# Retention's values centred per token, in place of a mean taken over the retention output

## The chip, the cores and the metric

The kernel runs on one core of a Trainium2 chip, as one launch. The metric is the device time in microseconds (us) of that core. The engines are named as in the profile: PE (TensorE), with PEld for its weight loads, DVE (VectorE), ACT (ScalarE), POOL (GpSimd) and SP (SyncE, which here only issues DMAs).

## The reference

Two decoder blocks over 512 tokens of width 1024, all in float32. The first has a retention layer, a chunked attention layer and two MLPs with a squared ReLU, the second a layer with three kinds of attention and a gated MLP. The change touches the retention layer only, which has 4 heads of key width 256 and value width 512:

```
q, k, v, g = split(h @ w_in)            # per head: q, k 512x256; v, g 512x512
q, k = rope(q), rope(k) / sqrt(256)
o = decayed_scores(q, k) @ v            # per head 512 tokens x 512 values; chunkwise in the reference
mu  = mean(o, axis=-1)                  # over the 512 values of a head, per token
var = mean((o - mu)**2, axis=-1)
o = (o - mu) * rsqrt(var + 1e-6) * gn_g
y = (silu(g) * o) @ w_out
```

Each output token is a weighted sum of value rows, so the mean of an output row over its 512 values is the same weighted sum of the means of the value rows.

## The kernel before

Matrix products are float32 in accuracy: each operand is rounded to a high part (hi) and the rest (lo), and each product is three matmuls, hi by hi, hi by lo and lo by hi (lines 590 to 592, `mm3`). The weights come from one stream of 354 units of 128x1024 floats, in a ring of four slots. SP loads a unit into `raw`, ACT rounds it into `w_hi` (L1189), DVE subtracts it into `w_lo` (L1753); this pair is called `split`, and it is done three units ahead of the unit that PE works on. Each engine has its program written out by hand in its own order; only semaphores tie them together. Engines work strictly in the order of their programs.

Projections make tiles of 128 features by 512 tokens that go to PSUM banks 0 and 1 in turn. PE may start a tile only when the tile two before it has been read (semaphore `tile_read`). V is made the other way round (`token_major`): 128 tokens by 512 values of a head, in banks 4 to 7.

The order of a retention head `ret_head` on PE is: four tiles for Q and K; four units of V; the output projection of the head before (`ret_out`, four units of two tiles each; the first head has none, the last has two here and two later); the four score products; the first tile of the gate G; P by V (L745 on) into banks 4 to 7; the other three tiles of G. With heads 1 and 2 in a loop and heads 0 and 3 written out.

Around V: when V stands in banks 4 to 7, ACT rounds each bank, scaled by the token's inverse norm (`rcol`), into `rv_h` (L1290, 4 instructions), and DVE makes `rv_l` from the bank and `rv_h` (L1912, 4 instructions). Behind these stands the next `split` of each engine, and behind that, on DVE, `out_tile`, which adds a tile of the output projection to `h` (L1811) and gives `tile_read`. The scores' third product uses bank 4 and so waits for `v_lo`; in head 0 it is P by V that waits for `v_lo`. P is rounded by ACT (L1298) and POOL takes its lo part (L2706). The semaphore `ret_p_lo` tells PE that POOL is done.

Around the group norm: ACT copies P by V from the banks to `oc` (L1308). POOL adds the four tiles of `oc` (L2711, L2715); inside the third gate tile PE multiplies that sum by a 128x128 matrix of ones (L759), which spreads the total over all partitions; DVE subtracts 1/512 of it from the four tiles of `oc` (L1933); ACT squares them into `sq` (L1314); POOL adds the squares (L2711, L2715 again); inside the fourth gate tile PE reduces them to a column per 128 tokens (L765); DVE and ACT make the inverse root (L1938, L1320, L1941, `make_diag` L1796 to L1801), PE spreads it (`gn_spread`, L658, L659) and DVE scales and gates (`y_scale` L1830, `y_gate` L1835).

Of the kernel before, what the change touches and what calls it, by code (L numbers as in the profile page):

```python
# [230 lines left out]
def build(nc, stream, x_t, cols, wf, f_bias, sinks, rel_pad, rel_2, c_rope, c_decay, c_sq, c_tri, c_sel,  # L231
# [4 lines left out]
    with ExitStack() as ctx:  # L236
# [38 lines left out]
        def f32(ap):  # L275
            return ap.bitcast(F32)
# [18 lines left out]
        m2, r_first = small[:, 2, 8:12], small[:, 2, 12:16]  # L295
        fl, fe, fn = small[:, 8, :], small[:, 9, :], small[:, 10, :]
        flog = small[:, 11, :]
        sums2 = [small[:, 4, 8 + 4 * n:12 + 4 * n] for n in range(2)]


# [36 lines left out]
        first_spread = sem("first_spread")  # L337
        h_normed = sem("h_normed")

        rope_tables = sem("rope_tables")  # L340
        rope_ready = sem("rope_ready")
        rope_hi = sem("rope_hi")
        rope_lo = sem("rope_lo")
        v_hi = sem("v_hi")
        v_lo = sem("v_lo")
        decay_landed = sem("decay_landed")
        ret_scores = sem("ret_scores")
        ret_p = sem("ret_p")
# [3 lines left out]
        ret_o = sem("ret_o")  # L352
        gn_sum = sem("gn_sum")
        gn_done = sem("gn_done")
        gn_centred = sem("gn_centred")
        gn_sq = sem("gn_sq")
        gn_ms_r = sem("gn_ms_r")
        gn_sd_r = sem("gn_sd_r")
# [71 lines left out]
        merge_a = sem("merge_a")  # L430
        merged = sem("merged")

        pad_made = sem("pad_made")
        conv_0 = sem("conv_0")
        conv_1 = sem("conv_1")
        conv_2 = sem("conv_2")
# [146 lines left out]
        def _(pe):  # L583
# [126 lines left out]
            def ret_head(hd, first, last=False):  # L710
                if first:
                    token_major(0, tiles=xl_ready)
                    strip_rows()
                    token_major(1, tiles=xl_ready)
                    proj(first=[(xl_ready, 0)], hooks={7: first_square})
                    proj(hooks={4: lambda: spread_rms(0)})
                else:
                    proj(hooks={5: lambda: gn_spread(hd - 1)})
                    proj()
                proj()  # L720
                proj()

                wait(pe, ret_o, hd * 4)
                for kk in range(2 if first else 0, 4):
                    token_major(kk)
                if not first:
                    wait(pe, y_lo, hd * 4)
                    for n in range(2 if last else 4):
                        ret_out(n)

                wait(pe, rope_lo, hd * 4 + 4)
                narrow = 1 if first else 4
                assert not first or at.t.b % 2 == 0
                if first:
                    wait(pe, tile_read, at.t)
                for j, (b, o) in enumerate([(2, 0), (3, 0), (narrow, 0), (narrow, 256)]):
                    if j == 2 and not first:
                        wait(pe, v_lo, hd * 4 + 4)
                    for d in range(2):
                        keys = (rqk_h[2 + d][:, j * P:j * P + P], rqk_l[2 + d][:, j * P:j * P + P])  # L740
                        m = mm3(banks[b][:, o:o + T_W[j]], keys, (rqk_h[d][:, j * P:S], rqk_l[d][:, j * P:S]),
                                d == 0, d == 1)
                    m.then_inc(ret_scores, 1)
                proj()

                if first:
                    wait(pe, v_lo, hd * 4 + 4)
                wait(pe, ret_p_lo, hd * 4 + 4)
                for c in range(4):
                    for j in range(TT):  # L750
                        val = (rv_h[j][:, c * P:c * P + P], rv_l[j][:, c * P:c * P + P])
                        sc = (rp_h[:, T_AT[j]:T_AT[j] + T_W[j]], rp_l[:, T_AT[j]:T_AT[j] + T_W[j]])
                        m = mm3(banks[4 + c][:, j * P:S], val, sc, j == 0, j == TT - 1)
                    m.then_inc(ret_pv, 1)
                proj()

                def mean():
                    wait(pe, gn_sum, hd * 6 + 3)
                    pe.matmul(banks[2][:, :], ones[:, :], acc[:, :], start=True, stop=True).then_inc(gn_done, 1)  # L759

                def variance():

                    wait(pe, gn_sum, hd * 6 + 6)
                    for t in range(TT):
                        m = pe.matmul(banks[3][:, t:t + 1], acc[:, t * P:t * P + P], ones[:, 0:1],  # L765
                                      start=True, stop=True)
                    m.then_inc(gn_done, 1)

                proj(hooks={3: mean})
                proj(hooks={6: variance})  # L770
                if last:
                    ret_out(2, hook=lambda: gn_spread(hd))
                    ret_out(3)
# [397 lines left out]
        def _(act):  # L1171
# [97 lines left out]
            def ret_head(hd, first, last=False):  # L1269
# [17 lines left out]
                value_splits(2 if first else 4)  # L1287
                wait(act, products_done, at.pe)
                for t in range(TT):
                    act.activation(rv_h[t], banks[4 + t][:, :], ACT.Copy, scale=rcol[:, t:t + 1]).then_inc(v_hi, 1)  # L1290
                if not first:
                    for _ in range(2 if last else 4):
                        split()
# [2 lines left out]
                for j in range(4):  # L1296
                    wait(act, ret_p, hd * 4 + (j + 1))
                    act.activation(rp_h[:, T_AT[j]:T_AT[j] + T_W[j]], pf_ret[:, T_AT[j]:T_AT[j] + T_W[j]],  # L1298
                                   ACT.Copy).then_inc(ret_p_hi, 1)
                at.step()  # L1300
                gate(hd, 0)
                split()
# [7 lines left out]
                gate(hd, 1)  # L1310
                split()
                for c in range(4):
                    wait(act, gn_centred, hd * 4 + (c + 1))
                    act.activation(sq[:, c, :], oc[c], ACT.Square).then_inc(gn_sq, 1)  # L1314
                at.step()
                gate(hd, 2)
# [419 lines left out]
        def _(dve):  # L1736
# [105 lines left out]

            def y_of(hd):

                wait(dve, gn_done, hd * 3 + 3)
                y_scale(hd, 0)
                y_scale(hd, 1)
                wait(dve, gate_ready, hd * 4 + 4)
                y_gate(hd, 0)
                y_scale(hd, 2)  # L1850
                y_gate(hd, 1)
                y_scale(hd, 3)
                y_gate(hd, 2)
                y_gate(hd, 3)
# [26 lines left out]
            def ret_head(hd, first, last=False):  # L1881
# [3 lines left out]
                if first:  # L1885
                    dve.wait_ge(squares_landed, 16)
                    rms(0)
                    dve.wait_ge(rbc_ready, 1)
                    dve.wait_ge(rope_landed, 32)
                    dve.tensor_tensor(cosr, cosr, rbc[:, :], ALU.mult)  # L1890
                    dve.tensor_tensor(sinr, sinr, rbc[:, :], ALU.mult).then_inc(rope_tables, 1)
                    dve.wait_ge(rope_tables, 1)

                    dve.wait_ge(masks_ready, 1)
                at.step()
# [12 lines left out]
                rotate(hd, 1, 1)  # L1908
                value_splits(2 if first else 4)
                for t in range(TT):  # L1910
                    wait(dve, v_hi, hd * 4 + (t + 1))
                    dve.scalar_tensor_tensor(rv_l[t], banks[4 + t][:, :], rcol[:, t:t + 1], f32(rv_h[t]),  # L1912
                                             ALU.mult, ALU.subtract).then_inc(v_lo, 1)
                if not first:
                    for n in range(2 if last else 4):
                        split()
# [9 lines left out]
                                      decay[:, 0:T_W[j]], ALU.mult).then_inc(ret_p, 1)  # L1926
                for c in range(4):
                    split()
                    if c == 2:

                        wait(dve, gn_done, hd * 3 + 1)
                        for e in range(4):
                            dve.scalar_tensor_tensor(oc[e], banks[2][:, :], -1.0 / RV, oc[e],  # L1933
                                                     ALU.mult, ALU.add).then_inc(gn_centred, 1)
                    if c == 3:

                        wait(dve, gn_done, hd * 3 + 2)
                        dve.tensor_scalar(gn_ms, banks[3][:, 0:4], 1.0 / RV, EPS, ALU.mult, ALU.add)\  # L1938
                            .then_inc(gn_ms_r, 1)
                        wait(dve, gn_sd_r, hd + 1)  # L1940
                        dve.reciprocal(gn_r, gn_sd).then_inc(gn_r_r, 1)  # L1941
                        wait(dve, gn_r_r, hd + 1)
                        make_diag(gn_r, gn_diag_h, gn_diag_l, gn_split, hd + 1).then_inc(gn_diag, 1)
                    at.step()
                    scaled(sg[c]).then_inc(tile_read, 1)
                if last:
                    split()
                    out_tile(4)
                    wait(dve, gn_done, hd * 3 + 3)
                    y_scale(hd, 0)  # L1950
                    y_scale(hd, 1)
                    wait(dve, gate_ready, hd * 4 + 4)
# [573 lines left out]

            for n in range(4):
                m = dve.memset(cz[n][:, 0:2], 0.0)
            m.then_inc(pad_made, 1)
            dve.wait_ge(pad_made, 1)  # L2530

            def taps(pair, n):

# [114 lines left out]
        def _(pool):  # L2648
# [45 lines left out]
            def ret_head(hd, first):  # L2694
# [11 lines left out]
                    pool.tensor_tensor(rp_l[:, a:a + w], pf_ret[:, a:a + w], f32(rp_h[:, a:a + w]), ALU.subtract)\  # L2706
                        .then_inc(ret_p_lo, 1)

                for k, (src, ready) in enumerate(((oc, ret_o), ([sq[:, c, :] for c in range(4)], gn_sq))):
                    wait(pool, ready, hd * 4 + 2)  # L2710
                    pool.tensor_tensor(acc[:, :], src[0], src[1], ALU.add).then_inc(gn_sum, 1)  # L2711
                    for c in (2, 3):
                        wait(pool, ready, hd * 4 + (c + 1))
                        wait(pool, gn_sum, hd * 6 + (3 * k + c - 1))
                        pool.tensor_tensor(acc[:, :], acc[:, :], src[c], ALU.add).then_inc(gn_sum, 1)  # L2715

            ret_head(Lin(0), True)
            with pool.Fori(0, RH - 1) as i:
# [290 lines left out]
```

## Time and profile before

| what | value |
|---|---|
| median of three runs | 2106.79 us (2106.16 to 2106.81) |
| the profiled execution, its own time | 2105.78 us |
| its span in the trace | 2104.1 us |
| PE busy | 2080.5 us, 99% of the span |
| DVE, ACT, POOL busy | 67%, 46%, 16% |
| the retention layer in the trace | from the start to about 421 us |

The span is what the trace covers; the execution's own time is 1.7 us longer. A timeline row gives start and duration in us, the engine, the line, the operation, the tiles written and read, and how long the engine had been idle before it and on whose account. A matmul's duration in the trace (0.39 us for 512 columns) overlaps that of the next one; the distance between two starts is what it costs.

### The profile page before, as it was taken

The page shows a single profiled execution, that of the slowest core. Times are in us where ns is not written, and L with a number is a line of the kernel's source. Part 1 is how long each engine was busy: PE and PEld are TensorE (multiplying, and loading weights), DVE is VectorE, ACT ScalarE, POOL GpSimd, SP SyncE. Part 2 cuts the span into 40 slices and gives each one's busy share as a digit, 9 for nine tenths or more (in the row PEclk, how much of TensorE's full clock was granted, in tenths as well). Part 3 has the DMA queues.
Part 4 walks back from the last instruction along what each step waited for, and adds up shares of the span by engine and source line. Part 5 has one row for each costly group of instructions (what it writes and reads, how often), then busy time and mean ns, then how long its engine had stood idle before and what let it go on. Part 6 is the DMA issues. An engine that isn't in the chain of part 4 may idle for free.

```text
span 2104.1 us, 30452 instructions
## 1 busy us (share of the span) xinstructions
PE 2080.5 (99%) x10614; PEld 1770.9 (84%) x10614; DVE 1403.4 (67%) x2320; ACT 978.2 (46%) x1652; POOL 330.1 (16%) x351
## 2 busy tenths in 40 slices
PE   8999999999999999999999999999999999999998
PEld 6888888789989888887899898878888888888887
DVE  6565554677868753887778687667765456666674
ACT  4433333464554344786645543457652244433342
POOL 4223132210001111443100002312310010000001
PEclk9999999999999999999999999999999999999999
DMA  5222213224234232222132232221222222333232
GB/s 195 84 92 76 100 65 100 70 71 155 99 106 146 97 104 85 91 90 76 61 131 90 100 112 99 96 90 53 76 83 100 100 90 96 109 103 113 99 104 67
DMA packets 58549, 203.77 MB, mean 97 GB/s; under 512 B 6937, under 2 KB 9129, under 8 KB 58448
## 3 DMA queue, kind: packets, MB, share of 16 engines
q1 hardware_dynamic: 54304, 189.82, 26.9%
q0 software_dynamic: 3712, 11.95, 1.9%
q8 instruction: 64, 1.05, 0.2%
q10 hardware_dynamic: 432, 0.66, 0.1%
q14 instruction: 37, 0.30, 0.0%
HBM read 200.27 MB, written 6.06 MB: 98 GB/s over the span
## 4 chain that ended last, share of the span: by engine, by line
PE 93%; ACT 3%; DVE 3%; issue 1%; DMA 0%; POOL 0%; ACTq 0%; DVEq 0%
PE bank L590 29%; PE bank L592 29%; PE bank L591 29%; PE bank L884 1%; PE bank L863 1%; ACT arena L1463 1%; PE bank L899 1%; PE bank L897 1%; DVE w_lo L1753 1%; PE bank L864 1%; ACT w_hi L1189 1%; ACT arena_r L1482 0%; ACT arena_r L1471 0%; DVE h L1811 0%; DMA colv<-in_cols 0%
## 5 line engine op out<-in xcount | busy, mean ns | idle before, releaser
L590 PE MATMUL bank<-x_hi,w_hi 128*128 128x512 f32 x1552 | 610.9, 394 | 1.4 <-issue 0.7
L591 PE MATMUL bank<-x_lo,w_hi 128*128 128x512 f32 x1560 | 608.0, 390 | 0.0
L592 PE MATMUL bank<-x_hi,w_lo 128*128 128x512 f32 x1552 | 605.3, 390 | 0.0
L1753 DVE TENSOR_TENSOR w_lo<-raw,w_hi 128x1024 fp32r<-128x1024 f32 x306 | 409.1, 1341 | 240.6 <-ACT w_hi L1189 240.3
L590 PE MATMUL bank<-arena_r,w_hi 128*128 128x256 f32 (+1 forms) x1328 | 440.1, 331 | 1.5 <-DVE h L1811 1.1
L592 PE MATMUL bank<-arena_r,w_lo 128*128 128x256 f32 (+1 forms) x1328 | 438.8, 330 | 0.0
L591 PE MATMUL bank<-arena_r,w_hi 128*128 128x256 f32 (+1 forms) x1312 | 432.6, 330 | 0.0
L1189 ACT ACTIVATE w_hi<-raw 128x1024 fp32r<-128x1024 f32 x306 | 320.0, 1051 | 192.6 <-PE bank L592 188.9
L590 PEld LDWEIGHTS bank<-x_hi,w_hi 128*128 128x128 f32 x1552 | 291.9, 188 | 62.4 <-issue 2.0
L591 PEld LDWEIGHTS bank<-x_lo,w_hi 128*128 128x128 f32 x1560 | 293.5, 188 | 60.2 <-issue 1.0
L592 PEld LDWEIGHTS bank<-x_hi,w_lo 128*128 128x128 f32 x1552 | 291.6, 188 | 61.5
L590 PEld LDWEIGHTS bank<-arena_r,w_hi 128*128 128x128 f32 x1328 | 252.4, 190 | 28.1 <-issue 2.9
L592 PEld LDWEIGHTS bank<-arena_r,w_lo 128*128 128x128 f32 x1328 | 252.4, 190 | 23.2
L591 PEld LDWEIGHTS bank<-arena_r,w_hi 128*128 128x128 f32 x1312 | 249.4, 190 | 22.3
L2750 POOL TENSOR_SCALAR arena<-arena,small 128x256 f32<-128x256 f32 (+3 forms) x128 | 89.5, 711 | 237.8 <-DVE small L2248 192.3
L1806 DVE TENSOR_TENSOR arena<-bank,rbc 128x512 f32<-128x512 f32 x77 | 53.0, 688 | 96.1 <-PE bank L592 96.0
L1811 DVE TENSOR_TENSOR h<-bank,h 128x512 f32<-128x512 f32 x96 | 65.6, 686 | 69.0 <-PE bank L592 68.9
L590 PE MATMUL bank<-w_hi,x_hi 128*128 128x512 f32 x224 | 88.2, 394 | 10.2 <-DVE x_lo L1759 9.3
L1359 ACT ACTIVATE w_hi<-raw 128x512 fp32r<-128x512 f32 x96 | 58.7, 623 | 77.8 <-PE bank L592 66.0
L1684 ACT ACTIVATE arena<-arena,colv 128x512 f32<-128x512 f32 x44 | 35.9, 817 | 124.6 <-DVE arena L1806 124.6
L2082 DVE TENSOR_TENSOR arena<-bank,arena 128x256 f32<-128x256 f32 x186 | 75.5, 417 | 23.4 <-PE bank L592 22.0
L591 PE MATMUL bank<-w_lo,x_hi 128*128 128x512 f32 x224 | 87.9, 393 | 0.0
(269 smaller groups left out, 2525.2 us busy)
## 6 DMA issues: line engine op xcount, KB each, us to landing
raw<-in_stream SPq DMA_DIRECT2D x354, 512.0 KB, 3.2
arena<-in_rel_pad POOLq DMA_DIRECT2D x16, 256.0 KB, 3.7
bias_strips<-bias_strip_once POOLq DMA_DIRECT2D x12, 320.0 KB, 4.3
out_t<-h SPq DMA_DIRECT2D x8, 256.0 KB, 2.2
h<-in_x_t SPq DMA_DIRECT2D x6, 256.0 KB, 8.4
arena<-in_c_decay POOLq DMA_DIRECT2D x4, 256.0 KB, 3.0
arena<-bias_strips POOLq DMA_DIRECT2D x4, 256.0 KB, 3.7
arena<-bias_strips POOLq DMA_DIRECT2D x8, 128.0 KB, 2.4
```

The source lines that it names most:

```text
L590: pe.matmul(dst, lh, rh, start=start, stop=False, **kw)
L591: pe.matmul(dst, lh, rl, start=False, stop=False, **kw)
L592: return pe.matmul(dst, ll, rh, start=False, stop=stop, **kw)
L863: pe.matmul(dst, q, kh_st[half][:, k0:k0 + w], start=True, stop=False, skip_group_check=True)
L1189: act.activation(w_hi[:, u % RING, :], raw[:, u % RING, :], ACT.Copy).then_inc(hi_ready, 1)
L1359: act.activation(block_at(slot)[0], src, ACT.Copy).then_inc(done, 1)
L1684: act.activation(cy[2 * (pair.b % 2) + n], cz[2 * (pair.b % 2) + n][:, 2:S + 2], ACT.Identity, scale=col(k + (C_CW + 2 * 2 * PAIRS)), bias ...
L1753: dve.tensor_tensor(w_lo[:, s, :], raw[:, s, :], f32(w_hi[:, s, :]), ALU.subtract).then_inc(lo_ready, 1)
L1806: return dve.tensor_tensor(dst, banks[(at.t - 1) % 2][:, :], rbc[:, :], ALU.mult)
L1811: dve.tensor_tensor(h[:, j, :], banks[(at.t - 1) % 2][:, :], h[:, j, :], ALU.add).then_inc(tile_read, 1)
L2082: dve.tensor_tensor(part, banks[bank][:, 0:QUARTER], part, ALU.add).then_inc(quarter_read, 1)
L2750: pool.tensor_scalar(pf[par][:, a:a + w], pf[par][:, a:a + w], rinv[par][:, t:t + 1], 1.0, ALU.mult, ALU.mult).then_inc(sm.probs, 1)
```

## The change

V is centred before it is rounded. ACT first copies each scaled bank of V to `sq` and has the instruction give the sum of each row as well (`accum_out`, into `v_sum`). DVE multiplies the sum by -1/512 (`v_neg`, one small instruction for each of the four token tiles). ACT then adds `v_neg` as a bias and rounds `sq` to `rv_h`, and DVE makes `rv_l` from `sq`, `v_neg` and `rv_h`. In heads 1 to 3 both follow at once. In head 0 ACT does it behind its rounding of P, and DVE behind the `split` of the first gate tile.

In the group norm the mean product on PE, POOL's three sums of `oc` and DVE's four subtractions go; ACT's squares stand where they stood and take `oc` as it was copied from the banks. The other edits only rename or recount semaphores.

```diff
@@ PE, ret_head
-                def mean():
-                    wait(pe, gn_sum, hd * 6 + 3)
-                    pe.matmul(banks[2][:, :], ones[:, :], acc[:, :], start=True, stop=True).then_inc(gn_done, 1)
...
-                    wait(pe, gn_sum, hd * 6 + 6)
+                    wait(pe, gn_sum, hd * 3 + 3)
...
-                proj(hooks={3: mean})
+                proj()
                 proj(hooks={6: variance})
@@ ACT, ret_head
                 for t in range(TT):
-                    act.activation(rv_h[t], banks[4 + t][:, :], ACT.Copy, scale=rcol[:, t:t + 1]).then_inc(v_hi, 1)
+                    act.activation(sq[:, t, :], banks[4 + t][:, :], ACT.Copy, scale=rcol[:, t:t + 1],
+                                   accum_out=v_sum[:, t:t + 1]).then_inc(v_scaled, 1)
+
+                def centred_his():
+                    for t in range(TT):
+                        wait(act, v_mean, hd * 4 + (t + 1))
+                        act.activation(rv_h[t], sq[:, t, :], ACT.Identity, bias=v_neg[:, t:t + 1]).then_inc(v_hi, 1)
+
+                if not first:
+                    centred_his()
                 if not first:
                     for _ in range(2 if last else 4):
                         split()
...
+                if first:
+                    centred_his()
                 at.step()
                 gate(hd, 0)
...
-                    wait(act, gn_centred, hd * 4 + (c + 1))
+                    wait(act, ret_o, hd * 4 + (c + 1))
                     act.activation(sq[:, c, :], oc[c], ACT.Square).then_inc(gn_sq, 1)
@@ DVE, ret_head
                 for t in range(TT):
-                    wait(dve, v_hi, hd * 4 + (t + 1))
-                    dve.scalar_tensor_tensor(rv_l[t], banks[4 + t][:, :], rcol[:, t:t + 1], f32(rv_h[t]),
-                                             ALU.mult, ALU.subtract).then_inc(v_lo, 1)
+                    wait(dve, v_scaled, hd * 4 + (t + 1))
+                    dve.tensor_scalar(v_neg[:, t:t + 1], v_sum[:, t:t + 1], -1.0 / RV, None, ALU.mult).then_inc(v_mean, 1)
+
+                def centred_los():
+                    for t in range(TT):
+                        wait(dve, v_hi, hd * 4 + (t + 1))
+                        dve.scalar_tensor_tensor(rv_l[t], sq[:, t, :], v_neg[:, t:t + 1], f32(rv_h[t]),
+                                                 ALU.add, ALU.subtract).then_inc(v_lo, 1)
+
+                if not first:
+                    centred_los()
...
                 for c in range(4):
                     split()
-                    if c == 2:
-
-                        wait(dve, gn_done, hd * 3 + 1)
-                        for e in range(4):
-                            dve.scalar_tensor_tensor(oc[e], banks[2][:, :], -1.0 / RV, oc[e],
-                                                     ALU.mult, ALU.add).then_inc(gn_centred, 1)
+                    if c == 0 and first:
+                        centred_los()
@@ POOL, ret_head
-                for k, (src, ready) in enumerate(((oc, ret_o), ([sq[:, c, :] for c in range(4)], gn_sq))):
-                    wait(pool, ready, hd * 4 + 2)
-                    pool.tensor_tensor(acc[:, :], src[0], src[1], ALU.add).then_inc(gn_sum, 1)
-                    for c in (2, 3):
...
+                wait(pool, gn_sq, hd * 4 + 2)
+                pool.tensor_tensor(acc[:, :], sq[:, 0, :], sq[:, 1, :], ALU.add).then_inc(gn_sum, 1)
+                for c in (2, 3):
...
```

## Rows read from the trace of the kernel before

**Rows 1.** The page: busy time of each engine.

```profile
PE 2080.5 (99%) x10614; PEld 1770.9 (84%) x10614; DVE 1403.4 (67%) x2320; ACT 978.2 (46%) x1652; POOL 330.1 (16%) x351
```

**Rows 2.** The waits of PE, whole span: us in total, times, longest.

```profile
PE bank L590 <- DVE x_lo L1759: 9.3, 1, 9.3
...
PE bank L1138 <- DVE diag L2615: 1.1, 1, 1.1
```

**Rows 3.** Timeline of PE around the mean product, head 0.

```profile
83.17 0.40 PE L592 MATMUL bank<-x_hi,w_lo 128*128 128x512 f32 x1
83.40 1.02 PE L759 MATMUL bank<-acc,ones 128*128 128x512 f32 x2
...
84.73 0.40 PE L592 MATMUL bank<-x_hi,w_lo 128*128 128x512 f32 x1
```

**Rows 4.** Timeline of ACT and of DVE behind V, head 1.

```profile
138.34 2.42 ACT L1290 ACTIVATE arena_r<-bank,small 128x512 fp32r<-128x512 f32 x4 [4.38 <-PE bank L592]
140.63 1.08 ACT L1189 ACTIVATE w_hi<-raw 128x1024 fp32r<-128x1024 f32 x1
...
141.74 1.23 DVE L1753 TENSOR_TENSOR w_lo<-raw,w_hi 128x1024 fp32r<-128x1024 f32 x1
142.88 0.68 DVE L1811 TENSOR_TENSOR h<-bank,h 128x512 f32<-128x512 f32 x1
```

**Rows 5.** Timeline of PE, the same stretch: second to third tile of `ret_out`.

```profile
143.35 0.39 PE L592 MATMUL bank<-arena_r,w_lo 128*128 128x512 f32 x1
143.71 0.47 PE L590 MATMUL bank<-arena_r,w_hi 128*128 128x512 f32 x1
```

**Rows 6.** Timeline of ACT in the attention layer: activations with accumulator output.

```profile
827.26 0.72 ACT L1463 ACTIVATE arena<-arena,small 128x512 f32<-128x512 f32 x1 [3.26 <-DVE small L2223]
827.89 0.18 ACT L1463 ACTIVATION_READ_ACCUMULATOR arena<-arena,small 128x1 f32 x1
827.98 0.60 ACT L1463 ACTIVATE arena<-arena,small 128x384 f32<-128x384 f32 x1
```

**Rows 7.** Timeline of ACT and of DVE behind the last output tiles.

```profile
410.67 0.73 ACT L1196 ACTIVATE x_hi<-h,colv 128x512 fp32r<-128x512 f32 x1
411.30 0.62 ACT L1204 ACTIVATE sq<-h 128x512 f32<-128x512 f32 x1
...
409.30 0.73 DVE L1759 SCALAR_TENSOR_TENSOR x_lo<-h,colv,x_hi 128x512 fp32r<-128x512 f32 x1
409.96 0.67 DVE L1811 TENSOR_TENSOR h<-bank,h 128x512 f32<-128x512 f32 x1
```

**Rows 8.** Timeline of POOL, DVE and PE, head 0, P's lo part.

```profile
64.90 2.00 POOL L2706 TENSOR_TENSOR arena_r<-arena,arena_r 128x384 fp32r<-128x384 f32 x1
66.85 1.15 POOL L2706 TENSOR_TENSOR arena_r<-arena,arena_r 128x256 fp32r<-128x256 f32 x2
...
63.82 2.20 DVE L1753 TENSOR_TENSOR w_lo<-raw,w_hi 128x1024 fp32r<-128x1024 f32 x1
...
68.15 0.47 PE L590 MATMUL bank<-arena_r 128*128 128x512 f32 x1
```

**Rows 9.** Timeline of POOL, head 1, the same operation.

```profile
164.45 1.02 POOL L2706 TENSOR_TENSOR arena_r<-arena,arena_r 128x384 fp32r<-128x384 f32 x1
```

**Rows 10.** Timeline of DVE, last head: centring, then the third gate tile.

```profile
377.66 2.48 DVE L1933 SCALAR_TENSOR_TENSOR arena<-bank,arena 128x512 f32<-128x512 f32 x4
380.52 0.69 DVE L1806 TENSOR_TENSOR arena<-bank,rbc 128x512 f32<-128x512 f32 x1 [0.38 <-PE bank L592]
```

**Rows 11.** Timeline of PE, the first matmuls of the kernel.

```profile
9.34 0.77 PE L590 MATMUL bank<-w_hi,x_hi 128*128 128x512 f32 x1 [9.34 <-DVE x_lo L1759]
...
13.30 0.39 PE L590 MATMUL bank<-w_hi,x_hi 128*128 128x512 f32 x1
13.53 0.40 PE L591 MATMUL bank<-w_lo,x_hi 128*128 128x512 f32 x1
```

**Rows 12.** Stages: busy us (instructions) of PE, PEld, DVE, ACT, POOL, then granted clock, DMA.

```profile
10.00:15.00 5.00, 5.00 (x17) 3.94 (x16) 4.54 (x4) 5.00 (x9) 4.29 (x3) 1.00 1.04 400
```

More of the change, by code:

```diff
@@ L297, in build @@
         flog = small[:, 11, :]
+        v_sum, v_neg = small[:, 8, 0:4], small[:, 9, 0:4]
         sums2 = [small[:, 4, 8 + 4 * n:12 + 4 * n] for n in range(2)]
@@ L338, in build @@
         h_normed = sem("h_normed")
-        rope_tables = sem("rope_tables")
+        tables_made = sem("tables_made")
         rope_ready = sem("rope_ready")
@@ L345, in build @@
         v_lo = sem("v_lo")
+        v_scaled = sem("v_scaled")
+        v_mean = sem("v_mean")
         decay_landed = sem("decay_landed")
@@ L354, in build @@
         gn_done = sem("gn_done")
-        gn_centred = sem("gn_centred")
         gn_sq = sem("gn_sq")
@@ L431, in build @@
         merged = sem("merged")
-        pad_made = sem("pad_made")
         conv_0 = sem("conv_0")
@@ L1843, in y_of @@
             def y_of(hd):
-                wait(dve, gn_done, hd * 3 + 3)
+                wait(dve, gn_done, hd * 2 + 2)
                 y_scale(hd, 0)
@@ L1890, in ret_head @@
                     dve.tensor_tensor(cosr, cosr, rbc[:, :], ALU.mult)
-                    dve.tensor_tensor(sinr, sinr, rbc[:, :], ALU.mult).then_inc(rope_tables, 1)
-                    dve.wait_ge(rope_tables, 1)
+                    dve.tensor_tensor(sinr, sinr, rbc[:, :], ALU.mult).then_inc(tables_made, 1)
+                    dve.wait_ge(tables_made, 1)
                     dve.wait_ge(masks_ready, 1)
@@ L1928, in ret_head @@
                     split()
-                    if c == 2:
-                        wait(dve, gn_done, hd * 3 + 1)
-                        for e in range(4):
-                            dve.scalar_tensor_tensor(oc[e], banks[2][:, :], -1.0 / RV, oc[e],
-                                                     ALU.mult, ALU.add).then_inc(gn_centred, 1)
+                    if c == 0 and first:
+                        centred_los()
                     if c == 3:
-                        wait(dve, gn_done, hd * 3 + 2)
+                        wait(dve, gn_done, hd * 2 + 1)
                         dve.tensor_scalar(gn_ms, banks[3][:, 0:4], 1.0 / RV, EPS, ALU.mult, ALU.add)\
@@ L1948, in ret_head @@
                     out_tile(4)
-                    wait(dve, gn_done, hd * 3 + 3)
+                    wait(dve, gn_done, hd * 2 + 2)
                     y_scale(hd, 0)
@@ L2528, in _ @@
                 m = dve.memset(cz[n][:, 0:2], 0.0)
-            m.then_inc(pad_made, 1)
-            dve.wait_ge(pad_made, 1)
+            m.then_inc(tables_made, 1)
+            dve.wait_ge(tables_made, 2)
             def taps(pair, n):
@@ L2707, in ret_head @@
                         .then_inc(ret_p_lo, 1)
-                for k, (src, ready) in enumerate(((oc, ret_o), ([sq[:, c, :] for c in range(4)], gn_sq))):
-                    wait(pool, ready, hd * 4 + 2)
-                    pool.tensor_tensor(acc[:, :], src[0], src[1], ALU.add).then_inc(gn_sum, 1)
-                    for c in (2, 3):
-                        wait(pool, ready, hd * 4 + (c + 1))
-                        wait(pool, gn_sum, hd * 6 + (3 * k + c - 1))
-                        pool.tensor_tensor(acc[:, :], acc[:, :], src[c], ALU.add).then_inc(gn_sum, 1)
+                wait(pool, gn_sq, hd * 4 + 2)
+                pool.tensor_tensor(acc[:, :], sq[:, 0, :], sq[:, 1, :], ALU.add).then_inc(gn_sum, 1)
+                for c in (2, 3):
+                    wait(pool, gn_sq, hd * 4 + (c + 1))
+                    wait(pool, gn_sum, hd * 3 + (c - 1))
+                    pool.tensor_tensor(acc[:, :], acc[:, :], sq[:, c, :], ALU.add).then_inc(gn_sum, 1)
             ret_head(Lin(0), True)
```

## The prediction

> **What bounds the kernel now.** I read the page's busy times first: PE is busy for 99% of the span, DVE for 67% [rows 1]. So a change is worth what it does to PE's program, and nothing that the other engines save counts unless PE waits for them. The waits of PE come next [rows 2]: after the 9.3 us at the start no single wait is over 1.1 us. That view can't show how near PE is to waiting where it doesn't wait. For that I read the timeline of each engine around the places that the diff touches.
>
> A matmul of 512 columns starts 0.23 us after the one before it (13.30 to 13.53) [rows 11]. At the third tile of `ret_out` the distance is 0.36 us, 143.35 to 143.71 [rows 5], so PE was held for 0.13 us. This tile may start when DVE has added the first one, and that addition ran from 142.88 to 143.56 [rows 4]. PE followed 0.15 us after its end. The profile calls this gap "issue", but the times fit `tile_read`: behind V, DVE is only just in time. Heads 2 and 3 run the same program, and I take them to be alike. Whatever delays DVE's first addition here delays PE by as much.
>
> **The mean product, removed.** From the L592 before it to the L592 behind it there are 1.56 us, in which three ordinary steps take 0.69 [rows 11]; the product costs PE 0.87 us [rows 3]. Four heads: **3.5 us gained**. The two records of L759 last 1.02 us; the price is not this duration but what the distance between starts leaves.
>
> **The three sums and four subtractions, removed.** The subtractions take DVE 2.48 us, and behind them DVE still waits 0.38 us for PE before it reads the third gate tile [rows 10]. PE hides them; taking them away gives nothing. If they were not hidden they would be worth up to 4 times 2.5 us, but then DVE would not be idle behind them. POOL is 16% busy, and the mean product started with no wait on POOL [rows 3]: nothing either. The fourth gate tile's reduction stays where it is, so the long chain through the inverse root starts at the same point of PE's program.
>
> **V in heads 1 to 3, in two passes.** I take head 1. ACT begins at 138.34; four copies last until the next instruction at 140.63, 0.57 us each [rows 4]. Now:
>
> - An accumulator output brings a second instruction. With it the next activation starts 0.72 us after the first [rows 6], where one of the same size with a pointer operand and no accumulator has a pitch of 0.63 (410.67 to 411.30) [rows 7]. It adds 0.09, so the scaled copies take 4 times 0.66, to 141.00.
> - The centring pass is four more activations from SBUF with a pointer operand, at 0.63 [rows 7], to 143.52. DVE's small products lie between and are hidden: the first is wanted 2 us after its sum exists.
> - ACT's split of the next unit starts then, and DVE's part follows 1.11 us after its start, as before (140.63 to 141.74), at 144.63. DVE's four low parts have two SBUF operands now and go at the pitch of such an instruction, 0.66 us (409.30 to 409.96) [rows 7]; the first can start when the first `rv_h` stands, 141.72, so they end at 144.4 and are ready just before the split.
> - DVE's split takes 1.14 us to the next start, the addition 0.68, and PE follows 0.15 later [rows 4, 5]: 146.60 in place of 143.71.
>
> The stall grows by **2.9 us** in each of three heads, 8.7 us. Later in the head it does not come again: the second addition follows at once, before PE has ended the third tile, and the splits are three units ahead. The scores' wait for `v_lo` is far behind in heads 1 and 2; in head 3 two units of `ret_out` (48 steps of 0.23, 11 us) still lie in front of it. The DMA queue is not held: the slot that SP fills waits on a split of an earlier unit.
>
> The bounds. Lower: the accumulator is free and the second pass is as quick as the first, 0.57. Then DVE's low parts end last, at 144.0, and PE starts at 146.0, 2.3 us late. Upper: nothing overlaps, each copy costs 0.72 + 0.18 and each centring 0.72; ACT's split then starts at 144.8, and PE is 4.2 us late. I take 2.9, as the rows with pointer operand and accumulator are the same instruction with another function.
>
> **V in head 0.** Here no `ret_out` covers it; P by V starts at 68.15, when POOL has the low parts of P (66.85 + 1.15 = 68.00) [rows 8]. The new low parts of V come behind DVE's split, from about 65.95. But DVE and POOL do not run side by side here: the split took 2.20 us where it takes 1.23 elsewhere [rows 4, 8], and POOL's 384 columns took 2.00 us where they take 1.02 in head 1 [rows 9]. One waits while the other works. From 65.95 on POOL has 0.95 + 1.15 us left and DVE four times 0.66; one after the other, in whatever order, the last ends at about 70.7, and PE starts at 70.85. **2.7 us lost.** If the two shared freely, DVE would end at 68.65 and the loss were 0.7; that is the lower bound, and 3.3 us the upper, if each change of hands costs 0.1 to 0.2 more.
>
> The Trainium skill (SBUF — State Buffer, the section "SBUF: two separate sides") says that a VectorE operation with two SBUF inputs and a GpSimd operation that reads SBUF lock each other out for the whole instruction. By that rule the old low part, with one input in PSUM, was free of it, and the new one is not: head 0 loses 2.7 us, and without the rule 0.7. The two stretched rows agree with it.
>
> **The sum.** -3.5 + 8.7 + 2.7 = +7.9 us. On the profiled execution's own 2105.78 us (span 2104.1 and 1.7 around it) that is 2113.7; the median of the runs shown lies 1.0 above that execution, so **2114.7 us**, 0.38% slower. With the lower bounds -3.5 + 6.9 + 0.7 = +4.1, 2110.9; with the upper ones -3.5 + 12.6 + 3.3 = +12.4, 2119.2.
>
> **Rivals.** *The third tile is not held by DVE.* The profile itself says "issue" for the 0.13 us; if PE's gate is something else, or DVE's addition goes ahead sooner, the second pass is hidden in heads 1 to 3. Place: the third tile of `ret_out`; the point from which it decides is a first addition that ends within 5.2 us of V's first copy. Then the time is 2106.8 - 3.5 + 2.7 = 2106.0, or 2103.3 if head 0's is hidden too. Against it: the step is longer than the 0.23 of its neighbours just there, and begins where the addition ends [rows 4, 5]. 1 in 10.
>
> *The clock of PE falls after the new gaps.* Nowhere behind the start has PE been idle for longer than 1.1 us [rows 2], and four gaps of 2.7 to 3 us would be new. At the start, after 9.3 us of idleness, nine steps take 3.96 us (9.34 to 13.30), 0.44 each, about what 512 columns take at 1.2 GHz, and from then on 0.23, at 2.4 GHz; the granted clock reads 1.00 in that stage all the same [rows 11, 12]. In place of 2.07 us, that is 1.9 us lost. Four times that gives 2114.7 + 7.6 = 2122.3. Gaps longer than 1.1 us are not in this trace behind the start. The Trainium skill (TensorE: Matmul & The Clock Gate, the table under "Why this matters for your kernels") warns that idle gaps between bursts of matmuls, of about the length forecast here, throw TensorE back to the lower clock; this would bring the 2122.3. No row here shows it. 7 in 100.
>
> *The stall lies between the two.* Say DVE gains an order in which half of the pass is hidden: below 2110.9 and above 2106. 3 in 100.
>
> **Numbers.** The forecast has 80 in 100 with its bounds 2110.9 to 2119.2, and with that I leave 2 in 10 outside. A measurement of this kernel tells 0.2% (4.2 us) from no change. Slower by that means above 2111.0: the forecast and the clock, 0.85. Same: most of the first rival and the third, 0.12. Faster needs less than 2102.6, more than the removed products are worth, 0.03.
>
> **What the profile after would show.** The waits of PE: L590 for DVE's L1811, three times some 2.9 us, and one of some 2.7 us at the start of P by V in head 0, for DVE's or POOL's low parts. No rows of the mean product, and 0.23 us steps across the third gate tile. ACT's group behind V about 5.2 us long where it was 2.4, with accumulator reads of 0.18. In head 0, low parts of V stretched or alternating with POOL's. The step between matmuls behind the gaps says whether the clock held. The prediction is wrong if the addition L1811 comes as early as before, if the second pass overlaps the first, or if the matmuls behind a gap are 0.43 us apart.

## The result, and the profile after

The changed kernel takes 2112.66 us (median of six runs, 2112.0 to 2117.93), against 2106.22 us for the kernel before in the runs beside it: the ratio is 1.0037, with a 95% interval of 1.0027 to 1.0048. It is slower, by 6.4 us in the medians. The span of the profiled execution grew from 2104.1 to 2110.6 us, by 6.5.

The waits of PE after show where. Each row has the time in all, the number of waits, and the longest (the lines have moved: L1819 is the addition to `h`, L1925 the low part of V, L1761 and L1186 the two halves of a split, L1287 and L1293 the two passes of ACT over V):

```profile
PE bank L591 <- DVE h L1819: 9.4, 6, 2.8
...
PE bank L591 <- DVE arena_r L1925: 1.7, 1, 1.7
```

The additions' row in the kernel before was

```profile
PE bank L590 <- DVE h L1811: 1.1, 3, 0.4
```

It now has three waits more, of 2.8 us each. The row of L1925 is new. The mean product had no row in this view even before: what it cost was PE's own work, not a wait, so its removal can't be seen here.

The timeline of ACT, DVE and PE behind V in head 1 answers to [rows 4, 5]:

```profile
138.92 0.69 ACT L1287 ACTIVATE sq<-bank,small 128x512 f32<-128x512 f32 x1 [4.38 <-PE bank L593]
139.51 0.19 ACT L1287 ACTIVATION_READ_ACCUMULATOR sq<-bank,small 128x1 f32 x1
139.60 0.68 ACT L1287 ACTIVATE sq<-bank,small 128x512 f32<-128x512 f32 x1
...
141.59 2.56 ACT L1293 ACTIVATE arena_r<-sq,small 128x512 fp32r<-128x512 f32 x4
144.05 2.00 ACT L1186 ACTIVATE w_hi<-raw 128x1024 fp32r<-128x1024 f32 x2
...
142.35 2.74 DVE L1925 SCALAR_TENSOR_TENSOR arena_r<-sq,small,arena_r 128x512 fp32r<-128x512 f32 x4 [0.46 <-ACT arena_r L1293]
145.13 1.23 DVE L1761 TENSOR_TENSOR w_lo<-raw,w_hi 128x1024 fp32r<-128x1024 f32 x1
146.27 1.28 DVE L1819 TENSOR_TENSOR h<-bank,h 128x512 f32<-128x512 f32 x2
...
143.94 0.39 PE L593 MATMUL bank<-arena_r,w_lo 128*128 128x512 f32 x1
147.10 0.47 PE L591 MATMUL bank<-arena_r,w_hi 128*128 128x512 f32 x1 [2.78 <-DVE h L1819]
```

Read it from ACT down. The pitch of a scaled copy is 0.66 or 0.67 us (138.92, 139.60) where it was 0.57; the second pass goes from 141.59 to 144.05; only then comes the split, then DVE's half of it, then the addition, and PE starts its third tile at 147.10. That is 8.18 us behind V's first copy, where it was 5.37 (138.34 to 143.71) [rows 4, 5]: 2.81 us more. This time the profile names the addition as the releaser. Heads 2 and 3 show the same gap of 2.78 us.

Behind the last of the three gaps there is more. PE in head 3, and the granted clock over stretches around it (the columns are those of [rows 12]):

```profile
353.25 0.47 PE L591 MATMUL bank<-arena_r,w_hi 128*128 128x512 f32 x1 [2.78 <-DVE h L1819]
...
354.51 0.63 PE L593 MATMUL bank<-arena_r,w_lo 128*128 128x512 f32 x1
354.94 0.63 PE L591 MATMUL bank<-arena_r,w_hi 128*128 128x512 f32 x1
...
357.90 0.40 PE L592 MATMUL bank<-arena_r,w_hi 128*128 128x512 f32 x1
```

```profile
346.00:350.00 4.00, 4.00 (x19) 3.33 (x18) 2.00 (x7) 4.00 (x10) 0.00 (x0) 1.00 0.00 0
353.00:358.00 5.00, 4.75 (x14) 3.78 (x15) 2.09 (x4) 0.00 (x0) 0.00 (x0) 0.66 0.64 212
358.00:362.00 4.00, 4.00 (x20) 3.31 (x19) 1.12 (x2) 1.06 (x1) 0.00 (x0) 1.00 0.00 1
```

From 354.51 to 357.90 the steps are 0.43 us, 512 columns at 1.2 GHz, and the granted clock is 0.66 over the stretch from 353 to 358; then they are 0.23 again. Ten steps from 354.02 to 357.90 took 3.88 us in place of 2.3: the clock cost 1.6 us here. Behind the other two gaps it held. The kernel before had such a fall too, at a place where PE had no gap, in the second block, behind a run of one-column matmuls:

```profile
1350.32 0.58 PE L652 MATMUL bank<-ones,arena 128*128 128x1 f32 x4
1350.77 0.47 PE L590 MATMUL bank<-x_hi,w_hi 128*128 128x512 f32 x1
...
1351.31 0.63 PE L592 MATMUL bank<-x_hi,w_lo 128*128 128x512 f32 x1
1351.74 0.63 PE L590 MATMUL bank<-x_hi,w_hi 128*128 128x512 f32 x1
```

The trace after has no fall there. So in these two traces a fall of 1.6 us stands on each side. At this place the clock fell in five of the nine traces (the kernel before and, of the experiments below, V's part alone, head 0's low parts ahead of the split, half of the passes moved, and the low parts from the bank) and held in the other four, though the change and the experiments leave this part of the program as it was.

### The profile page after: what moved, and what is told of

Its sections match the earlier page's. It is cut to its first block, busy times and chain, and to the rows that moved or that the text cites. A ratio compares the mean times of both kernels' runs of the same rounds, so it can differ in the third digit from the quotient of the medians.

```text
span 2110.6 us, 30442 instructions
## 1 busy us (share of the span) xinstructions
PE 2077.6 (98%) x10606; PEld 1769.0 (84%) x10606; DVE 1395.1 (66%) x2320; ACT 987.8 (47%) x1684; POOL 315.5 (15%) x339
## 4 chain that ended last, share of the span: by engine, by line
PE 93%; ACT 3%; DVE 3%; issue 1%; DMA 0%; POOL 0%; DVEq 0%; ACTq 0%
PE bank L591 29%; PE bank L593 29%; PE bank L592 29%; PE bank L881 1%; PE bank L860 1%; PE bank L896 1%; DVE w_lo L1761 1%; PE bank L861 1%; PE bank L894 1%; ACT w_hi L1186 1%; ACT arena L1471 1%; ACT sq L1287 1%; ACT arena_r L1293 0%; DVE h L1819 0%; ACT arena_r L1490 0%
## 5 line engine op out<-in xcount | busy, mean ns | idle before, releaser
L1761 DVE TENSOR_TENSOR w_lo<-raw,w_hi 128x1024 fp32r<-128x1024 f32 x306 | 406.4, 1332 | 239.3 <-ACT w_hi L1186 238.9
L1186 ACT ACTIVATE w_hi<-raw 128x1024 fp32r<-128x1024 f32 x306 | 319.6, 1051 | 193.5 <-PE bank L593 190.2
L1819 DVE TENSOR_TENSOR h<-bank,h 128x512 f32<-128x512 f32 x96 | 65.5, 687 | 72.5 <-PE bank L593 72.4
```

What stands on the lines that cost most here:

```text
L1186: act.activation(w_hi[:, u % RING, :], raw[:, u % RING, :], ACT.Copy).then_inc(hi_ready, 1)
L1761: dve.tensor_tensor(w_lo[:, s, :], raw[:, s, :], f32(w_hi[:, s, :]), ALU.subtract).then_inc(lo_ready, 1)
L1819: dve.tensor_tensor(h[:, j, :], banks[(at.t - 1) % 2][:, :], h[:, j, :], ALU.add).then_inc(tile_read, 1)
```

## The experiments

All times are medians beside runs of the kernel before on the same chip, 2105.91 us; ratios have their 95% interval.

**The group norm's part alone.** The kernel before, less everything that the change takes from the group norm:

```diff
-                proj(hooks={3: mean})
+                proj()
...
-                        for e in range(4):
-                            dve.scalar_tensor_tensor(oc[e], banks[2][:, :], -1.0 / RV, oc[e],
-                                                     ALU.mult, ALU.add).then_inc(gn_centred, 1)
```

> The kernel before, without the mean product on PE, without POOL's three sums of oc and without DVE's four subtractions. V is not centred either, so this kernel leaves out the centring of the group norm. My theory: only the product lay on PE's path, 0.87 us in each of 4 heads, so -3.5 us, about 2102.7 (ratio 0.9983), with the step between matmuls at 0.23 us across the third gate tile. Rival: DVE's 2.5 us of subtractions and POOL's sums were not wholly covered; then it gains more than 3.5 us, up to 4 x 3.4 = 13 us.

Measured: 2102.15 us, ratio 0.9982 (0.9973 to 0.9991), 3.8 us less. PE walks through the third gate tile without a step longer than 0.23:

```profile
84.13 0.39 PE L592 MATMUL bank<-x_hi,w_lo 128*128 128x512 f32 x1
84.36 0.39 PE L590 MATMUL bank<-x_hi,w_hi 128*128 128x512 f32 x1
84.58 0.39 PE L591 MATMUL bank<-x_lo,w_hi 128*128 128x512 f32 x1
```

The 3.5 us of the product are there, and the subtractions and sums are worth nothing that can be told apart from it (the interval is some 2 us wide on each side).

**V's part alone.** The changed kernel with the mean product, the sums and the subtractions put back:

```diff
-                proj()
+                proj(hooks={3: mean})
```

> The kernel after, with the mean product, the sums and the subtractions put back (they then subtract a mean that is zero but for rounding). My theory: all of the loss is in V's second pass: three gaps of 2.8 us on PE and 1.5 us in head 0, +9.9 us, about 2116, and 1.6 us more for each gap after which the clock falls. Rival: the loss comes from what the removal did (squares and sums sooner, other meetings of DVE and POOL); then this kernel is no more than 3.5 us above the one before.

Measured: 2120.21 us, ratio 1.0068 (1.0054 to 1.0082), 14.3 us more. The trace has the same three gaps of 2.78 us and one of 1.65 in head 0, some 10 us in all, and behind two of the three the clock fell; this is the second:

```profile
252.24 0.68 PE L591 MATMUL bank<-arena_r,w_hi 128*128 128x512 f32 x1 [2.78 <-DVE h L1823]
252.72 0.63 PE L592 MATMUL bank<-arena_r,w_hi 128*128 128x512 f32 x1
253.14 0.63 PE L593 MATMUL bank<-arena_r,w_lo 128*128 128x512 f32 x1
```

10.0 + 2 x 1.6 = 13.2, near the 14.3; the span of this trace is 13.6 us longer than that of the kernel before, and each of the two has a fall behind the one-column matmuls besides. The two parts alone, -3.8 and +14.3, make 10.5 where the whole change made 6.4. Falls of the clock explain most of the 4.1 us between them: the mean granted clock is known for every execution, and it is 0.996 in four of these five, where the trace has three falls, and 0.998 in four of the changed kernel's six, where the trace has one. Two falls more are 3.2 us. Why this kernel has them more often isn't known.

**The passes moved behind the first addition.** No work added or taken; in heads 1 to 3 only the order changes:

```diff
@@ ACT
+                if not first:
+                    split()
                 wait(act, products_done, at.pe)
...
@@ DVE
-                if not first:
-                    centred_los()
                 if not first:
                     for n in range(2 if last else 4):
-                        split()
+                        if n:
+                            split()
                         for c in range(2):
                             out_tile(2 * n + c)
+                            if n == 0:
+                                centred_los(range(2 * c, 2 * c + 2))
```

(DVE's first split stands ahead of the `v_neg` products.)

> The kernel after, with one thing moved: in heads 1 to 3 ACT's and DVE's split of the next unit, and the first addition to h, go ahead of the centring passes, whose low parts are then made two behind each of the first two additions. No work is added or taken. My theory: PE's third tile is held by the addition behind the passes, so the three gaps go: 2106.2 - 3.5 + 1.5 = 2104.2 (ratio 0.9990), no PE gap by the addition over 0.2 us in heads 1 to 3, and no fall of the clock there. Rival: PE waits because ACT and DVE have more work in all behind V; then the gaps move to the fourth or fifth tile or to the scores and the time stays near 2112.

Measured: 2103.91 us, ratio 0.9989 (0.9980 to 0.9998). The waits of PE, and PE across the second and third tile in head 1, where the gap was:

```profile
PE bank L591 <- DVE arena_r L1930: 1.6, 1, 1.6
...
PE bank L591 <- DVE h L1822: 1.1, 3, 0.4
```

```profile
143.64 0.39 PE L592 MATMUL bank<-arena_r,w_hi 128*128 128x512 f32 x1
143.87 0.39 PE L593 MATMUL bank<-arena_r,w_lo 128*128 128x512 f32 x1
144.10 0.39 PE L591 MATMUL bank<-arena_r,w_hi 128*128 128x512 f32 x1
144.32 0.39 PE L592 MATMUL bank<-arena_r,w_hi 128*128 128x512 f32 x1
```

The additions' row is back at what it was before the change. The third tile starts at 144.10, 0.23 us behind the step before it, so the hold of 0.13 us that the kernel before had there [rows 5] is gone too. The same passes cost nothing when the addition doesn't stand behind them. The rival that it was the amount of work is out. The traced execution, at 2101.43 us the quickest of the eleven, has no fall of the clock at all (granted clock 0.999); those at 2104 us and more have 0.998 or 0.997.

**In head 0 the low parts ahead of the split.**

```diff
                 for c in range(4):
-                    split()
                     if c == 0 and first:
                         centred_los()
+                    split()
```

> As e3_passes_later, and in head 0 DVE makes the low parts of V ahead of its split. My theory: that split of 1.1 us is taken out of the turns that DVE and POOL take, so P by V starts some 1.1 us sooner: about 2103.1. Rival: POOL's low parts of P end last then, pushed back by DVE, or ACT's rounding of V (its last ends at about 66.4 in the trace after) sets the start; then 0.3 us or less is gained, about 2104.

Measured: 2102.22 us, ratio 0.9982 (0.9973 to 0.9991). DVE and PE in head 0:

```profile
64.87 4.01 DVE L1930 SCALAR_TENSOR_TENSOR arena_r<-sq,small,arena_r 128x512 fp32r<-128x512 f32 x4 [1.24 <-ACT arena_r L1295]
68.81 1.21 DVE L1764 TENSOR_TENSOR w_lo<-raw,w_hi 128x1024 fp32r<-128x1024 f32 x1
...
68.94 0.50 PE L591 MATMUL bank<-arena_r 128*128 128x512 f32 x1 [0.68 <-DVE arena_r L1930]
```

The gap shrinks from 1.64 to 0.68 us, by 1.0 where 1.1 was expected; the low parts could not start until ACT's first `rv_h` stood (DVE idle for 1.24 us). The median fell by 1.7 us, more than the gap did; the executions of the kernel without this step already spread from 2101.4 to 2104.7 us, so of the medians' difference only the gap's 1.0 us is accounted for. This kernel beats both: 3.7 us less than the kernel before, 10 less than the change as made.

**Longer gaps.** One more DVE product behind the low parts, which nobody reads:

```diff
                 if not first:
                     centred_los()
+                    dve.tensor_tensor(f_at(2, 4), f32(x_hi[:, 0:4, :]).rearrange("p k n -> p (k n)"),
+                                      f32(x_lo[:, 0:4, :]).rearrange("p k n -> p (k n)"), ALU.mult)
```

> The kernel after, with one product of 2048 elements more on DVE behind the low parts of V in heads 1 to 3; nobody reads its result. My theory: DVE's first addition comes some 2 us later still, PE's three gaps grow from 2.8 to about 4.8 us, and now the clock falls behind each of the three, 1.6 us each (seven matmuls at 0.43 us in place of 0.23): 2106 - 3.5 + 1.5 + 3 x (4.8 + 1.6) = 2123. Rival: the fall seen in the kernel after has nothing to do with the gap (it stood at another place of the kernel before, with no gap); then the three gaps grow, the clock falls once or not at all in the trace, and the time is 2118 to 2120.

Measured: 2124.16 us, ratio 1.0086 (1.0069 to 1.0102). The first of the three gaps, and the clock before, behind and later:

```profile
150.19 0.77 PE L591 MATMUL bank<-arena_r,w_hi 128*128 128x512 f32 x1 [4.85 <-DVE h L1819]
150.75 0.63 PE L592 MATMUL bank<-arena_r,w_hi 128*128 128x512 f32 x1
151.18 0.63 PE L593 MATMUL bank<-arena_r,w_lo 128*128 128x512 f32 x1
```

```profile
140.00:144.00 4.00, 4.00 (x19) 3.34 (x18) 1.25 (x5) 4.00 (x11) 0.00 (x0) 1.00 0.02 4
150.00:155.00 5.00, 4.82 (x11) 3.80 (x12) 1.77 (x3) 0.00 (x0) 0.00 (x0) 0.50 0.66 210
156.00:160.00 4.00, 4.00 (x19) 3.31 (x18) 1.53 (x3) 1.06 (x1) 0.00 (x0) 1.00 0.00 0
```

All three gaps of 4.85 us are followed by matmuls at the lower level, 10, 6 and 12 records of 0.62 to 0.63 us. These 28 steps cost some 0.2 us each, 5.6 us in all, where I had forecast 4.8. The extra product took DVE 2.2 us, and the gaps grew by 2.07. So a microsecond of DVE here costs PE very nearly a microsecond, and these gaps cost the clock as well, each time.

**Half of the passes moved.** ACT and DVE centre two token tiles ahead of the split and two behind it:

```diff
-                    centred_los()
+                    centred_los(range(2))
...
+                        if n == 0:
+                            centred_los(range(2, 4))
```

> The kernel after, with only two of the four token tiles centred ahead of the split and the first additions in heads 1 to 3, and the other two behind them. My theory: two activations of 0.63 us leave the chain to the first addition, so the gaps shrink from 2.8 to about 1.5 us, and the clock does not fall behind them: 2106 - 3.5 + 1.5 + 3 x 1.5 = 2108.6. Rival: whether a gap is long does not matter to the clock; then some of these gaps too are followed by matmuls at 0.43 us, and the time is 1.6 us more for each.

Measured: 2108.69 us, ratio 1.0014 (1.0004 to 1.0023). Head 1:

```profile
145.70 0.47 PE L591 MATMUL bank<-arena_r,w_hi 128*128 128x512 f32 x1 [1.56 <-DVE h L1821]
146.00 0.40 PE L592 MATMUL bank<-arena_r,w_hi 128*128 128x512 f32 x1
146.24 0.39 PE L593 MATMUL bank<-arena_r,w_lo 128*128 128x512 f32 x1
```

Three gaps of 1.56 us (the third 1.57), none followed by a slow step. With gaps of 1.6, 2.8 and 4.85 us in heads 1 to 3 the clock fell behind none of three, behind three of six (two traces), and behind three of three. Nor did it fall behind head 0's gap of 1.65 us, which five traces have.

**Head 0's low parts from the bank.** The same instruction with one SBUF input instead of two, on top of the kernel with the passes moved:

```diff
+                        if first:
+                            dve.scalar_tensor_tensor(rv_l[t], banks[4 + t][:, :], rcol[:, t:t + 1], f32(rv_h[t]),
+                                                     ALU.mult, ALU.subtract).then_inc(v_lo, 1)
+                            continue
```

> As e3_passes_later, but in head 0 the low parts of V are taken from V's PSUM bank, as in the kernel before (so rv_l of head 0 leaves out the mean; the rest computes as before). The instruction is as long, with one SBUF input in place of two. My theory: with two SBUF inputs DVE and POOL take turns, with one they don't, so the four low parts take 2.7 us in place of 4.2, POOL's four 4.4 in place of 5.3, and PE begins P by V some 1.4 us sooner, nearly without a gap: 2102.6. Rival: head 0's gap is only the order of DVE's work behind its split; then the low parts stay stretched to 4 us, PE's gap stays at 1.6 us, and the time at 2104.

Measured: 2101.65 us, ratio 0.9978 (0.9969 to 0.9988). First DVE and POOL operation by operation in the changed kernel, head 0:

```profile
65.38 1.51 DVE L1925 SCALAR_TENSOR_TENSOR arena_r<-sq,small,arena_r 128x512 fp32r<-128x512 f32 x1
66.81 1.22 DVE L1925 SCALAR_TENSOR_TENSOR arena_r<-sq,small,arena_r 128x512 fp32r<-128x512 f32 x1
...
64.34 2.00 POOL L2718 TENSOR_TENSOR arena_r<-arena,arena_r 128x384 fp32r<-128x384 f32 x1
66.30 1.18 POOL L2718 TENSOR_TENSOR arena_r<-arena,arena_r 128x256 fp32r<-128x256 f32 x1
67.44 0.90 POOL L2718 TENSOR_TENSOR arena_r<-arena,arena_r 128x128 fp32r<-128x128 f32 x1
...
69.61 0.50 PE L591 MATMUL bank<-arena_r 128*128 128x512 f32 x1 [1.65 <-DVE arena_r L1925]
```

and the same stretch with the bank as source:

```profile
65.92 2.71 DVE L1931 SCALAR_TENSOR_TENSOR arena_r<-bank,small,arena_r 128x512 fp32r<-128x512 f32 x4
...
63.61 4.38 POOL L2728 TENSOR_TENSOR arena_r<-arena,arena_r 128x512 fp32r<-128x512 f32 x4 [9.83 <-ACT arena_r L1307]
...
68.69 0.50 PE L591 MATMUL bank<-arena_r 128*128 128x512 f32 x1 [0.19 <-DVE arena_r L1931]
```

Above, each operation is as long as it takes to wait for the other engine's and then do its own: DVE's first low part lasts 1.51 us and ends 0.55 us after POOL's 384 columns (66.34). Below, four low parts take 2.71 us in place of 4.17, and POOL's four 4.38 in place of 5.27. PE's gap falls from 1.65 to 0.19 us. So the turns come from the second SBUF input, not from the order on DVE. (The time fell by 2.3 us against the kernel with the passes moved, more than the 1.45 of the gap; the rest is not traced to a cause.)

## Why the prediction was right

It said 2114.7 us, between 2110.9 and 2119.2; it was 2112.66, 6.4 us slower where 7.9 were forecast.

- *The bound and the edge.* DVE's first addition was the thing to look at, though the wait view had it at nothing. Moving it took the gaps away, and the 0.13 us with them; lengthening the chain by 2 us lengthened them by 2. So the 0.13 us were the wait for the addition, whatever the profile called them; the first rival is out.
- *The mean product*, 3.5 us: the part alone gave 3.8.
- *Subtractions and sums*, nothing: the same experiment, within its interval.
- *V in heads 1 to 3*, 2.9 us each: 2.8 in each. Its parts: copies with accumulator 0.66 forecast, 0.66 to 0.67 measured; centring 0.63, measured 2.46 us to the split for four; split and addition as before.
- *V in head 0*, 2.7 us: this term was mis-sized. P by V started at 69.61, and V's first copy in that trace 0.12 us earlier than before, so the loss was 1.6 us. I had DVE enter the low parts at 65.95, as in the trace before. But there the old low parts of V stood ahead of DVE's products for P, which started at 62.23; after, only small instructions stand there and they start at 61.64, so that the low parts begin at 65.38. Those 0.6 us (0.5, counted from V's first copy) were DVE work that the change took away, and I left them out. The rest: I put DVE's and POOL's times end to end, and the turns overlap. From 65.38 on POOL had 0.96 + 1.16 us left and DVE 2.71, the last two as they are with the bank as source, 4.83 in all; it took 4.17, by this estimate 0.6 or 0.7 less. That they take turns, and why, was right. The trace agrees with the rule of the Trainium skill that the prediction drew on (SBUF — State Buffer, "SBUF: two separate sides") in which pairs of instructions take turns. It does not agree that one is kept out for the whole of the other: the first low part ends 0.55 us behind POOL's operation, where alone it lasts 0.74 (65.92, with the bank as source).
- *The clock.* I gave its fall behind the gaps 7 in 100, for all four. It came in part: behind one gap of three in the trace after, two of three with V's part alone, never in head 0. The rival was too coarse, all or none, and it looked for the clock at the start only: the fall at 1351 us, in the trace of the kernel before, was missed. In the sum, the one fall that came stands against that one, and that they cancel in these two traces is luck, not foresight; without the fall at 1351 on the other side the difference would have been about 8 us, still inside the range. Such falls may also be why the six runs spread over 6 us: the execution of 2117.93 us has a mean granted clock of 0.995, those near 2112 have 0.998. Which gaps they were isn't known, since only one was traced. The Trainium skill's warning of idle gaps between bursts of matmuls (TensorE: Matmul & The Clock Gate, "Why this matters for your kernels") agrees with these traces in kind: the clock did fall behind gaps. But it reads as a plain limit, where gaps of 2.78 us were followed by a fall in three of six cases, and it says nothing of a fall like that at 1351 us, with no gap.
- *The sum*, on the two spans: -3.5 + 3 x 2.8 + 1.6 - 0.1 (the earlier start) = +6.4, with the fall in head 3 against the fall at 1351 us; measured +6.5. So head 0's term, 1.1 us too large, is what the forecast of 7.9 was mainly off by.

## What to carry to other kernels

A wait view shows who waits, not who is about to: where an engine is released just as it needs it, as PE was here, which was held for 0.13 us, anything put ahead of the releasing instruction lands on the bound engine nearly in full, and anything put behind it may be free. So when a change adds work off the bound engine, look up which instruction in that queue frees a buffer, and put the new work behind it: here the same instructions gave +6.4 us in one order and -3.7 in another. And count what the change takes out of a queue ahead of the critical instruction, too.

## What the runs showed of the hardware that I had not expected

- A gap of 2.8 us on PE is followed by a fall of the clock only sometimes: three of six in two traces of the same order of work. When it falls it may do so at the first matmul behind the gap (252.24 in V's part alone) or five steps later (354.51 in the changed kernel).
- PE need not be idle for it: one-column matmuls alone, 2.6 us of them with no gap, preceded the fall at 1351 us in the kernel before. The same matmuls preceded a fall in four other traces and none in four.
- The granted clock of the page's 40 slices reads 9 throughout, in the slices with a fall too; only a stretch of some 5 us shows the 0.66 and the 0.50.
